# Sums of weights made by an adding DMA, and activation words turned by one DMA, in the feed-forward of a two-layer decoder on one Trainium2 core

## The chip, the cores and the metric

The kernel runs on one core of one Trainium2 chip. The metric is the device time of one execution in microseconds. In the trace PE is TensorE, PEld its weight load, DVE VectorE, ACT ScalarE, POOL GpSimd and SP SyncE; ACTq and SPq are DMAs being issued by ACT and by SP. PE ran at its full granted clock all through the profiled execution.

## The reference

Two pre-norm residual layers on 256 tokens of width 2048, each with an attention part and a SwiGLU feed-forward of width 5632. The change touches the feed-forward alone:

```python
def swiglu(h, w_gate, w_up, w_down):
    return (jax.nn.silu(h @ w_gate) * (h @ w_up)) @ w_down
```

Everything is float32. `h` is 256 x 2048, `w_gate` and `w_up` are 2048 x 5632, `w_down` is 5632 x 2048, for each of the two layers.

## The kernel before

**Products in three parts.** PE multiplies rounded 32-bit values. So each weight value and each activation is held as a high part (rounded, made by ACT, L1115) and a low part (what the rounding lost, made by DVE, L1379), and each product is three matmuls: high x high, high x low, low x high (`three`, L1757). ACT's and DVE's main work is this splitting of weights. A weight chunk of 128 x 2048 values (1 MB) comes into one of `RAW` = 4 slots of `raw`, and is split in halves of 128 x 1024 into a ring of `SPLIT` = 4 slots, `w_hi` and `w_lo`. ACT may write slot s when PE is done with the half that lies four back in the order; DVE follows ACT; SP loads a chunk into a `raw` slot when DVE is done with what was there. In the walk, the loop that all engines follow, the half that ACT splits at a step is `AHEAD` = 3 halves ahead of the one PE multiplies, and DVE's is 2 ahead.

**The feed-forward in column blocks.** `w_gate` and `w_up` are taken in 11 blocks of 512 columns. The first goes through two plain passes. For the other ten the two matrices go together: 8 chunks for each block, one for each pair k of row tiles (a, b), with up and gate side by side. The four 128 x 512 parts of a chunk lie as 0 = up rows a, 1 = gate rows a, 2 = up rows b, 3 = gate rows b. The body of a round takes them in the order k = 4, 5, 6, 7 of one block and then 0, 1, 2, 3 of the next (`BODY`). Six of the eight are "eights": two halves, 24 matmuls of 512 columns. Two, k = 4 (f = 0) and k = 7 (f = 1), are "sevens": the 2 x 2 blocks of weights are multiplied with seven products instead of eight, 21 matmuls, in four parts of 6, 3, 6 and 6 matmuls (`seven_part`, L1763). The parts need as weights: "two" = parts 2 and 3 of the chunk, "one" = part 1, "sums_a" = two sums, "sums_b" = the other two sums. The sums of weights are made by DVE in `make_sums` (L1382), in three steps: step 0 writes gate_a + up_a and up_b + up_a in one instruction (L1392) into `sums[2:4]`, which is "sums_b"; steps 1 and 2 (L1397) add up_b and then gate_b to the first of these, which gives "sums_a". The walk puts the steps ahead of the part that needs them: those of f = 0 at i = 4, 5, 6 of the four eights k = 0 to 3, those of f = 1 at i = 0, 1, 2 of the eights k = 5, 6. The matching sums of the activations (`form_hi`, `form_lo`) are made once for each layer. The seven products are put together again by ACT and DVE in `direct_out` and `mix`, during the second seven and the eights behind it. One round of the body (8 chunks, 186 matmuls of 512 columns) takes 44.2 us; there are nine such rounds in each layer, 18 in all.

**The hidden activations turned.** The result of a block, `hid`, must be turned for the product with `w_down`. DMAs turn 2-byte words only, so DVE splits the 4-byte values into two planes of words (`hidden_words`, L1707), ACT issues four transposing DMAs of 128 x 512 words each into `wordsT` (`hidden_turn`, L1344; L1350), and DVE merges the words into `hT` (`hidden`, L1717; L1722). In each round the turn stands at i = 3 of the eights k = 5, 6: in ACT's order it lies between the splits of "sums_a" and "sums_b" of the second seven. The memory of `words` is used again by ACT in `mix(0)`, which waits for the turn. There is one more turn behind the rounds of each layer and one in the first rows of the product with `w_down`.

**Other places that turn words.** In the attention parts SP issues transposing DMAs of 128 x 2048 words as one instruction (`turn_nat` L927, `turn_x` L939), which is the same size as the four of `hidden_turn` together.

**POOL** has little to do: small loads at the start, powers for the norms, and ten copies in the first layer's attention. In the rounds of the feed-forward it does nothing.

Of the kernel before, what the change touches and what calls it, by code (L numbers as in the profile page):

```python
# [22 lines left out]
P = 128  # L23
# [62 lines left out]
class Counts:  # L86


    def __init__(self):
# [6 lines left out]
        self.mix = Count()  # L96
        self.direct = Count()
# [15 lines left out]
    def loop(self, eng, rounds, sets=(0, 0), **per):  # L113

        known = {"half": self.half, "chunk": self.chunk, "made": self.made, "raw": self.raw, "up": self.up,
                 "sums": self.sums, "mix": self.mix, "direct": self.direct, "norm": self.norm, "qkT": self.qkT, "pair": self.pair,
# [97 lines left out]
def decoder_kernel(nc, widths, x_in, attn_norm, ffn_norm, even_w_in, even_q_norm, even_k_norm, even_sinks,  # L214
# [27 lines left out]
    with ExitStack() as ctx:  # L242
# [14 lines left out]
        with ExitStack() as s0:  # L257
            sums = sb("sums", [P, 4, NB], F32, s0)
        with ExitStack() as s1:
# [6 lines left out]
            wordsT = sb("wordsT", [P, 2, 4, SEQ], U16, s1)  # L266
            form_hi = sb("form_hi", [P, len(SEVENS), 4, P], F32R, s1)
            form_lo = sb("form_lo", [P, len(SEVENS), 4, P], F32R, s1)
        shared = words[:, :, :, :].rearrange("p w m n -> p (w m n)").bitcast(F32).rearrange("p (m n) -> p m n", n=NB)
        xs_sum = sums[:, 0:2, :].rearrange("p f (t s) -> p f t s", t=2)  # L270
        forms = sums[:, 2:4, :].rearrange("p f (c q) -> p f c q", q=P)
# [18 lines left out]
        bias = sb("bias", [P, 2, 2, S384], F32)  # L290
        t_two = sb("t_two", [P, 2, S384], F32)
        tri_r = sb("tri_r", [P, P], F32R)
        n_wordsT = sb("n_wordsT", [P, 2, MT, 4, P], U16)
# [29 lines left out]
        up_loaded = [sem(f"up_loaded{i}") for i in range(4)]  # L323
        sums_made = sem("sums_made")
# [108 lines left out]
        def split_views(kind, s, r):  # L433
# [7 lines left out]
            if kind in ("sums_a", "sums_b"):  # L441
                at = 0 if kind == "sums_a" else 2
                return HALF, sums[:, at:at + 2, :].rearrange("p a n -> p (a n)")
            return HALF, chunk[:, (r % 2) * HALF:(r % 2 + 1) * HALF]

        def split_over(n, kind):
# [3 lines left out]
            if kind != "plain":  # L450
                n.up.c += raw_halves

# [3 lines left out]
        def walk(eng, e):  # L456
# [151 lines left out]
            def feed_forward(layer):  # L608
# [38 lines left out]
                def make_sums(step, f, more):  # L647
                    e.sums(step, f, more)
# [23 lines left out]
                def sums_ahead(i):  # L672
                    if i in (4, 5, 6):
                        make_sums(i - 4, 0, 1 if i == 4 else 0)

                def body(j, more):

                    def middle(i):
                        if i < 3:
                            make_sums(i, 1, 1 if i == 0 else 0)  # L680
# [5 lines left out]
                    def tail(i):  # L686
# [3 lines left out]
                        if more:  # L690
                            sums_ahead(i)
# [9 lines left out]
                eights(range(FIRST_K), PARTS["seven"][:AHEAD], sums_ahead)  # L701
                with n.loop(eng, FB - 3, half=len(KINDS), made=len(KINDS), raw=16, up=16, sums=2, mix=1, direct=1, sets=(0, 2),
# [179 lines left out]
        def _(sp):  # L882
# [14 lines left out]
            def pair_chunk(layer, k, cols, halves, freed):  # L897
# [5 lines left out]
                for w, of, loaded in ((1, w_gate, raw_loaded[s]), (0, w_up, up_loaded[u])):  # L903
                    sp.dma_start(dst[:, w, :, :],
                                 of[layer][rows, cols].rearrange("(t p) n -> p t n", p=P)).then_inc(loaded, 16)
                n.chunk.c += 1
                n.up.c += 1
                n.half.c += halves
# [62 lines left out]
            def feed_forward(layer):  # L971
# [4 lines left out]
                for k in range(FIRST_K):  # L976
                    pair_chunk(layer, k, slice(NB, 2 * NB), 2, 2 * (RAW - 1))
                with n.loop(sp, FB - 2, chunk=8, up=8, half=whole) as j:
                    for i, of in enumerate(BODY):
                        k = (FIRST_K + i) % len(BODY)  # L980
                        freed = begins[i] - ends[i - RAW] + (whole if i < RAW else 0)
                        pair_chunk(layer, k, bass.ds(j * NB + (NB if k >= FIRST_K else 2 * NB), NB), len(PARTS[of]), freed)
                for k in range(FIRST_K, KT // 2):
                    pair_chunk(layer, k, slice((FB - 1) * NB, FB * NB), 2, 2 * (RAW - 1))
# [65 lines left out]
        def _(pool):  # L1050
# [41 lines left out]
            e = Steps(begin=begin, rms=rms, norm_b=norm_b, nat_words=nat_words)  # L1092
# [4 lines left out]
        def _(act):  # L1097
            def split(kind="plain"):
# [11 lines left out]
                if kind in ("sums_a", "sums_b"):  # L1110
                    act.wait_ge(sums_made, n.sums.value(unit=3))
                if n.made.past(SPLIT):
                    act.wait_ge(half_used, n.made.value(1 - SPLIT))
                out, src = split_views(kind, s, r)
# [871 lines left out]
```

## Time and profile before

| | us |
|---|---|
| median of 3 runs | 2169.42 (2167.51 to 2169.66) |
| the profiled execution, own time | 2165.94 |
| its span, first to last instruction | 2163.8 |
| PE busy | 2125.5 (98%) |
| DVE busy | 1490.3 (69%) |
| ACT busy | 1190.5 (55%) |
| POOL busy | 65.6 (3%) |
| DMA queues together, share of the 16 engines' time | 63.6% |
| moved by DMA | 442.35 MB |
| chain that ended last | PE 92%, ACTq 4%, DVE 2%, ACT 1% |

A matmul of 512 columns is shown with 389 ns, but one begins every 0.227 us: they overlap, and a busy PE here is a PE whose matmuls follow each other without a gap. Busy shares of the other engines say little, since each only has to keep ahead of PE.

### The profile page before, as it was taken

The page shows a single profiled execution, that of the slowest core. Times are in us where ns is not written, and L with a number is a line of the kernel's source. Part 1 is how long each engine was busy: PE and PEld are TensorE (multiplying, and loading weights), DVE is VectorE, ACT ScalarE, POOL GpSimd, SP SyncE. Part 2 cuts the span into 40 slices and gives each one's busy share as a digit, 9 for nine tenths or more (in the row PEclk, how much of TensorE's full clock was granted, in tenths as well). Part 3 has the DMA queues.
Part 4 walks back from the last instruction along what each step waited for, and adds up shares of the span by engine and source line. Part 5 has one row for each costly group of instructions (what it writes and reads, how often), then busy time and mean ns, then how long its engine had stood idle before and what let it go on. Part 6 is the DMA issues. An engine that isn't in the chain of part 4 may idle for free.

```text
span 2163.8 us, 28900 instructions
## 1 busy us (share of the span) xinstructions
PE 2125.5 (98%) x9859; PEld 1750.9 (81%) x9859; DVE 1490.3 (69%) x1957; ACT 1190.5 (55%) x1630; POOL 65.6 (3%) x39
## 2 busy tenths in 40 slices
PE   9999999999999999999999999999999999999999
PEld 8888888777777778888888888888777777788887
DVE  5775667788788766555667676776788878865555
ACT  6676656455554544444557576664555545544443
POOL 1101000000000000000011001000000000000000
PEclk9999999999999999999999999999999999999999
DMA  7776456656666576555567777765666665665553
GB/s 277 226 225 208 166 184 206 203 195 206 191 208 209 186 203 210 192 192 192 179 210 236 232 226 241 237 206 196 193 206 208 197 213 185 214 206 194 193 193 136
DMA packets 301851, 442.35 MB, mean 204 GB/s; under 512 B 134640, under 2 KB 137424, under 8 KB 291024
## 3 DMA queue, kind: packets, MB, share of 16 engines
q1 hardware_dynamic: 253488, 429.76, 60.4%
q10 hardware_dynamic: 47968, 11.58, 3.1%
q8 instruction: 46, 0.75, 0.1%
q14 instruction: 29, 0.24, 0.0%
q0 software_dynamic: 320, 0.02, 0.0%
HBM read 408.27 MB, written 2.10 MB: 190 GB/s over the span
## 4 chain that ended last, share of the span: by engine, by line
PE 92%; ACTq 4%; DVE 2%; ACT 1%; issue 0%; DMA 0%; SPq 0%; DVEq 0%
PE acc L1759 16%; PE acc L1760 15%; PE acc L1761 15%; PE work L1759 14%; PE work L1761 14%; PE work L1760 14%; ACTq L1350 4%; DVE w_lo L1379 1%; PE work L1909 1%; ACT w_hi L1115 1%; PE work L1947 1%; PE work L1859 0%; DMA raw<-in_even_w_in_dram 0%; PE work L1920 0%; PE work L1954 0%
## 5 line engine op out<-in xcount | busy, mean ns | idle before, releaser
L1115 ACT ACTIVATE w_hi<-raw 128x1024 fp32r<-128x1024 f32 x756 | 777.3, 1039 | 589.3 <-PE work L1761 360.1
L1379 DVE TENSOR_TENSOR w_lo<-raw,w_hi 128x1024 fp32r<-128x1024 f32 x756 | 897.0, 1196 | 178.9 <-ACT w_hi L1115 176.0
L1759 PE MATMUL work<-w_hi,xT_hi 128*128 128x512 f32 x1064 | 414.5, 390 | 0.0
L1761 PE MATMUL work<-w_hi,xT_lo 128*128 128x512 f32 x1064 | 414.2, 389 | 0.0
L1760 PE MATMUL work<-w_lo,xT_hi 128*128 128x512 f32 x1064 | 414.2, 389 | 0.0
L1759 PE MATMUL acc<-w_hi,xT_hi 128*128 128x512 f32 (+1 forms) x836 | 325.6, 389 | 1.1 <-DVE w_lo L1379 1.1
L1761 PE MATMUL acc<-w_hi,xT_lo 128*128 128x512 f32 (+1 forms) x836 | 322.2, 385 | 0.0
L1760 PE MATMUL acc<-w_lo,xT_hi 128*128 128x512 f32 (+1 forms) x836 | 322.1, 385 | 0.0
L1759 PEld LDWEIGHTS work<-w_hi,xT_hi 128*128 128x128 f32 x1064 | 200.0, 188 | 42.0 <-DVE w_lo L1379 0.4
L1760 PEld LDWEIGHTS work<-w_lo,xT_hi 128*128 128x128 f32 x1064 | 200.0, 188 | 41.7
L1761 PEld LDWEIGHTS work<-w_hi,xT_lo 128*128 128x128 f32 x1064 | 199.9, 188 | 41.6
L1759 PEld LDWEIGHTS acc<-w_hi,xT_hi 128*128 128x128 f32 x836 | 157.0, 188 | 36.7 <-DVE w_lo L1379 3.0
L1379 DVE TENSOR_TENSOR w_lo<-sums,w_hi 128x1024 fp32r<-128x1024 f32 x72 | 88.2, 1226 | 139.5 <-ACT w_hi L1115 138.2
L1761 PEld LDWEIGHTS acc<-w_hi,xT_lo 128*128 128x128 f32 x836 | 157.1, 188 | 31.8
L1760 PEld LDWEIGHTS acc<-w_lo,xT_hi 128*128 128x128 f32 x836 | 157.2, 188 | 30.2
L1115 ACT ACTIVATE w_hi<-sums 128x1024 fp32r<-128x1024 f32 x72 | 76.4, 1061 | 184.5 <-PE work L1761 105.1
L1728 DVE TENSOR_TENSOR stage_lo<-hT,stage_hi 128x256 fp32r<-128x256 f32 x88 | 37.4, 425 | 156.5 <-ACT stage_hi L1359 156.5
L1759 PE MATMUL work<-w_hi,stage_hi 128*128 128x512 f32 x352 | 137.2, 390 | 0.5 <-DVE hid L1702 0.5
L1759 PE MATMUL acc<-w_hi,stage_hi 128*128 128x512 f32 x352 | 137.0, 389 | 0.1
L1761 PE MATMUL work<-w_hi,stage_lo 128*128 128x512 f32 x352 | 137.0, 389 | 0.0
L1760 PE MATMUL acc<-w_lo,stage_hi 128*128 128x512 f32 x352 | 137.0, 389 | 0.0
L1761 PE MATMUL acc<-w_hi,stage_lo 128*128 128x512 f32 x352 | 136.9, 389 | 0.0
(176 smaller groups left out, 2420.2 us busy)
## 6 DMA issues: line engine op xcount, KB each, us to landing
raw<-in_ffn_w_down_dram SPq DMA_DIRECT2D x88, 1024.0 KB, 4.8
raw<-in_ffn_w_gate_dram SPq DMA_DIRECT2D x160, 512.0 KB, 3.6
raw<-in_ffn_w_up_dram SPq DMA_DIRECT2D x160, 512.0 KB, 4.5
raw<-in_odd_w_in_dram SPq DMA_DIRECT2D x48, 1024.0 KB, 5.6
raw<-in_even_w_in_dram SPq DMA_DIRECT2D x32, 1024.0 KB, 5.7
raw<-in_even_w_out_dram SPq DMA_DIRECT2D x16, 1024.0 KB, 5.0
raw<-in_odd_w_out_dram SPq DMA_DIRECT2D x16, 1024.0 KB, 5.8
bias<-in_bias_dram SPq DMA_DIRECT2D x24, 384.0 KB, 3.7
```

What stands on the lines that cost most here:

```text
L1115: act.activation(w_hi[:, s, 0:out], src, ACT.Copy).then_inc(hi_ready, 1)
L1350: act.dma_start_transpose(wordsT[:, w, :, m * P:(m + 1) * P], words[:, w, m, :]).then_inc(wordsT_loaded, 16)
L1379: dve.tensor_tensor(w_lo[:, s, 0:out], src, w_hi[:, s, 0:out].bitcast(F32), ALU.subtract).then_inc(lo_ready, 1)
L1728: dve.tensor_tensor(stage_lo[:, t, :], hT[:, bass.ds(kt, 1), :].rearrange("p a b -> p (a b)"), stage_hi[:, t, :].bitcast(F32), ALU.subtrac ...
L1759: pe.matmul(out_ps, x_hi, wh, start=start, stop=False)
L1760: pe.matmul(out_ps, x_hi, wl, start=False, stop=False)
L1761: return pe.matmul(out_ps, x_lo, wh, start=False, stop=stop)
L1909: last = pe.matmul(o[rows[b], m, :], v_nat[:, k, h * HD:(h + 1) * HD], pt[:, b, (k + m) * P:(k + m + 1) * P], start=first, stop=stop)
L1947: last = pe.matmul(banks[:, b, lo:hi], qT[rows[b], j % 4, m * P:(m + 1) * P], kT[rows[b], key, 0:hi - lo], start=True, stop=True)
```

## The change

Two independent edits, both in the feed-forward.

First, `hidden_turn` issues one transposing DMA of 128 x 2048 words instead of four of 128 x 512. The destination `wordsT` is laid out (plane, token tile, feature tile, token) to suit, and `hidden` reads it in that order.

Second, the two sums of "sums_b" are made by DMA. For a seven SP no longer loads up_a into `raw`; it loads gate and up_b as before, and loads gate_a and up_b once more into a buffer of their own, `near[f]`. POOL waits for these two loads and issues a DMA that reads up_a twice from the weights in memory and adds it to both parts of `near[f]`. "sums_b" is split from `near[f]`. DVE's step 0 is gone; its step 1 waits for the adding DMA and makes up_b + (gate_a + up_a) into `far[1]`, step 2 adds gate_b into `far[0]`, and "sums_a" is split from `far`. The buffer `bias` moves behind `tri_r` in memory.

```diff
@@ hidden_turn, hidden (ACT, DVE)
-                for w in range(2):
-                    for m in range(MT):
-                        act.dma_start_transpose(wordsT[:, w, :, m * P:(m + 1) * P],
-                                                words[:, w, m, :]).then_inc(wordsT_loaded, 16)
+                act.dma_start_transpose(wordsT[:, :, :, :, :].rearrange("p w m t q -> p (w m t) q"),
+                                        words[:, :, :, :].rearrange("p w m n -> p (w m n)")).then_inc(wordsT_loaded, 16)
@@
-                    last = dve.tensor_copy(pairs.rearrange("p (n w) -> p n w", w=2)[:, :, w],
-                                           wordsT[:, w, :, :].rearrange("p a q -> p (a q)"))
+                    last = dve.tensor_copy(whole[:, :, :, :, w], wordsT[:, w, :, :, :].rearrange("p m a q -> p a m q"))
@@ pair_chunk (SP)
+                if of == "eight":
+                    sp.dma_start(dst[:, 0, :, :],
+                                 w_up[layer][rows, cols].rearrange("(t p) n -> p t n", p=P)).then_inc(up_loaded[u], 16)
+                else:
+                    a, b = (slice((2 * k + t) * P, (2 * k + t + 1) * P) for t in range(2))
+                    f = SEVENS.index(k)
+                    sp.dma_start(dst[:, 0, 1, :], w_up[layer][b, cols]).then_inc(up_loaded[u], 16)
+                    sp.wait_ge(flo_ready, layer + 1)
+                    sp.dma_start(near[:, f, 0, :], w_gate[layer][a, cols]).then_inc(near_loaded[f], 16)
+                    sp.dma_start(near[:, f, 1, :], w_up[layer][b, cols]).then_inc(near_loaded[f], 16)
@@ POOL
+            def add_near(step, j, more, layer):
+                if step == 0:
+                    f, at = e.n.sums.slot(2), 2 * SEVENS[e.n.sums.slot(2)] * P
+                    pool.wait_ge(near_loaded[f], e.n.sums.turn(2, plus=1, unit=32))
+                    pool.nop(nofuse=True)
+                    pool.dma_start(near[:, f, :, :],
+                                   w_up[layer][at:at + P, bass.ds(j * NB + NB, NB)].unsqueeze(1).broadcast_to([P, 2, NB]),
+                                   accum_op=ALU.add).then_inc(near_added[f], 16)
@@ make_sums (DVE)
-                if step == 0:
-                    dve.wait_ge(lo_ready, n.made.value((-7, -3)[f]))
-                    dve.wait_ge(flo_ready, n.ffn.value())
+                if step == 1:
+                    dve.wait_ge(lo_ready, n.made.value(-(7, 3)[f] - 1))
+                    dve.wait_ge(near_added[f], n.sums.turn(2, plus=1, unit=16))
                     dve.wait_ge(raw_loaded[n.raw.slot(2 * RAW, more) // 2], n.raw.turn(2 * RAW, more, plus=1, unit=16))
                     dve.wait_ge(up_loaded[n.up.slot(2 * RAW, more) // 2], n.up.turn(2 * RAW, more, plus=1, unit=16))
-                    dve.tensor_tensor(sums[:, 2:4, :], chunk[:, 1:3, :],
-                                      chunk[:, 0:1, :].broadcast_to([P, 2, NB]), ALU.add).then_inc(sums_made, 1)
-                else:
-                    dve.wait_ge(sums_made, n.sums.value(unit=3) + step)
-                    out, a, b = ((1, sums[:, 2, :], chunk[:, 2, :]), (0, sums[:, 1, :], chunk[:, 3, :]))[step - 1]
-                    dve.tensor_tensor(sums[:, out, :], a, b, ALU.add).then_inc(sums_made, 1)
+                    dve.tensor_tensor(far[:, 1, :], near[:, f, 0, :], chunk[:, 2, :], ALU.add).then_inc(sums_made, 1)
+                if step == 2:
+                    dve.wait_ge(sums_made, n.sums.value(unit=2) + 1)
+                    dve.tensor_tensor(far[:, 0, :], far[:, 1, :], chunk[:, 3, :], ALU.add).then_inc(sums_made, 1)
```

## Rows read from the trace of the kernel before

**Rows 1.** The page's part 1, the engine line of PE.
```profile
PE 2125.5 (98%) x9859; PEld 1750.9 (81%) x9859; DVE 1490.3 (69%) x1957; ACT 1190.5 (55%) x1630; POOL 65.6 (3%) x39
```

**Rows 2.** Groups by line: busy us, mean ns | idle before, releaser.
```profile
L1759 PE MATMUL acc<-w_hi,form_hi 128*128 128x512 f32 x108 | 44.3, 411 | 31.7 <-DVE w_lo L1379 31.7
...
L1392 DVE TENSOR_TENSOR sums<-raw 128x1024 f32<-128x1024 f32 x36 | 43.9, 1219 | 0.0
```

**Rows 3.** Waits of PE, whole span: us in total, times, longest.
```profile
PE acc L1759 <- DVE w_lo L1379: 32.8, 20, 1.9
```

**Rows 4.** Timeline, one turn: start us, us, engine, line, operation [idle before].
```profile
539.49 5.19 ACTq L1350 DMA_TRANSPOSE wordsT<-words  x4
...
541.66 0.39 PE L1761 MATMUL work<-w_hi,xT_lo 128*128 128x512 f32 x1
...
544.80 1.06 ACT L1115 ACTIVATE w_hi<-sums 128x1024 fp32r<-128x1024 f32 x1 [4.38 <-PE acc L1761]
...
545.89 1.23 DVE L1379 TENSOR_TENSOR w_lo<-sums,w_hi 128x1024 fp32r<-128x1024 f32 x1 [4.21 <-ACT w_hi L1115]
...
547.17 0.50 PE L1759 MATMUL acc<-w_hi,form_hi 128*128 128x512 f32 x1 [1.72 <-DVE w_lo L1379]
```

**Rows 5.** Line L1350: issue ns shortest/median/longest, first and last start.
```profile
L1350 ACTq DMA_TRANSPOSE wordsT<-words x88: 1207/1299/1859, 406.8 to 1933.0; - x88
```

**Rows 6.** Line L927, SP's wide turns of the same size, same columns.
```profile
L927 SPq DMA_TRANSPOSE n_wordsT<-sq x13: 1322/1615/6267, 89.2 to 1336.9; - x13
```

**Rows 7.** Timeline of SP around a slow and a fast wide turn.
```profile
109.59 0.45 SPq L893 DMA_DIRECT2D raw<-in_even_w_in_dram  x1
110.39 5.88 SPq L927 DMA_TRANSPOSE n_wordsT<-sq  x1
...
1193.01 1.32 SPq L927 DMA_TRANSPOSE n_wordsT<-sq  x1
```

**Rows 8.** Timeline of SP through one round of the body.
```profile
506.48 0.37 SPq L904 DMA_DIRECT2D raw<-in_ffn_w_gate_dram  x1
...
510.30 0.37 SPq L904 DMA_DIRECT2D raw<-in_ffn_w_gate_dram  x1
...
518.37 0.37 SPq L904 DMA_DIRECT2D raw<-in_ffn_w_gate_dram  x1
...
538.97 0.37 SPq L904 DMA_DIRECT2D raw<-in_ffn_w_gate_dram  x1
539.44 0.42 SPq L904 DMA_DIRECT2D raw<-in_ffn_w_up_dram  x1
```

**Rows 9.** DMA issues: count, KB each, median us from issue to landing.
```profile
raw<-in_ffn_w_gate_dram SPq DMA_DIRECT2D x160, 512.0 KB, 3.6
raw<-in_ffn_w_up_dram SPq DMA_DIRECT2D x160, 512.0 KB, 4.5
...
sinks<-in_even_sinks_dram POOLq DMA_DIRECT2D x1, 8.0 KB, 5.5
```

**Rows 10.** Timeline of DVE from the sums of f = 0 to their split.
```profile
518.12 0.69 DVE L1397 TENSOR_TENSOR sums<-sums,raw 128x512 f32<-128x512 f32 x1
...
524.82 1.23 DVE L1379 TENSOR_TENSOR w_lo<-sums,w_hi 128x1024 fp32r<-128x1024 f32 x1
...
534.58 0.68 DVE L1397 TENSOR_TENSOR sums<-sums,raw 128x512 f32<-128x512 f32 x1
```

**Rows 11.** Timeline of PE: the first matmul that needs "sums_a" of f = 0.
```profile
528.28 0.39 PE L1759 MATMUL work<-w_hi,xT_hi 128*128 128x512 f32 x1
```

**Rows 12.** Timeline of POOL and DVE: a DMA issue, and POOL beside DVE.
```profile
6.07 0.58 POOL L1060 DMA_DIRECT2D sinks<-in_even_sinks_dram  x1
...
350.14 1.22 DVE L1379 TENSOR_TENSOR w_lo<-raw,w_hi 128x1024 fp32r<-128x1024 f32 x1
...
350.31 1.60 POOL L1066 TENSOR_TENSOR rstd<-msq,half 128x2 f32<-128x2 f32 x1 [142.29 <-DVE msq L1550]
...
1077.83 0.70 POOL L1066 TENSOR_TENSOR rstd<-msq,half 128x2 f32<-128x2 f32 x1 [725.91 <-DVE msq L1550]
```

More of the change, by code:

```diff
@@ L96, in __init__ @@
         self.mix = Count()
+        self.unit = Count()
         self.direct = Count()
@@ L257, in decoder_kernel @@
         with ExitStack() as s0:
-            sums = sb("sums", [P, 4, NB], F32, s0)
+            near = sb("near", [P, 2, 2, NB], F32, s0)
         with ExitStack() as s1:
@@ L323, in decoder_kernel @@
         up_loaded = [sem(f"up_loaded{i}") for i in range(4)]
+        near_loaded = [sem(f"near_loaded{i}") for i in range(2)]
+        near_added = [sem(f"near_added{i}") for i in range(2)]
         sums_made = sem("sums_made")
@@ L440, in split_views @@
                 return NB, chunk[:, NB:HALF]
-            if kind in ("sums_a", "sums_b"):
-                at = 0 if kind == "sums_a" else 2
-                return HALF, sums[:, at:at + 2, :].rearrange("p a n -> p (a n)")
+            if kind == "sums_a":
+                return HALF, far[:, :, :].rearrange("p a n -> p (a n)")
+            if kind == "sums_b":
+                return HALF, near[:, unit, :, :].rearrange("p a n -> p (a n)")
             return HALF, chunk[:, (r % 2) * HALF:(r % 2 + 1) * HALF]
@@ L451, in split_over @@
                 n.up.c += raw_halves
+            if kind == "sums_b":
+                n.unit.c += 1
         TURNS_B = ((19, (31, 32), 35, q_nat, qT, NA // 2), (32, (38, 39), None, k_nat, kT, NA // 2),
@@ L645, in stage, with make_sums @@
                     n.kt.c += 1
-                def make_sums(step, f, more):
-                    e.sums(step, f, more)
+                def make_sums(step, j, more):
+                    e.sums(step, j, more, layer)
                     if step == 2:
@@ L699, in body @@
                     n.sets[1].c += 2
-                eights(range(FIRST_K), PARTS["seven"][:AHEAD], sums_ahead)
-                with n.loop(eng, FB - 3, half=len(KINDS), made=len(KINDS), raw=16, up=16, sums=2, mix=1, direct=1, sets=(0, 2),
+                eights(range(FIRST_K), PARTS["seven"][:AHEAD], lambda i: sums_ahead(0, i))
+                with n.loop(eng, FB - 3, half=len(KINDS), made=len(KINDS), raw=16, up=16, sums=2, unit=2, mix=1, direct=1, sets=(0, 2),
                             hT=1) as j:
@@ L895, in chunk, with pair_chunk @@
                 n.half.c += 2
-            def pair_chunk(layer, k, cols, halves, freed):
+            def pair_chunk(layer, k, of, cols, freed):
                 sp.wait_ge(lo_ready, n.half.value(-freed))
@@ L902, in pair_chunk @@
                 rows = slice(2 * k * P, (2 * k + 2) * P)
-                for w, of, loaded in ((1, w_gate, raw_loaded[s]), (0, w_up, up_loaded[u])):
-                    sp.dma_start(dst[:, w, :, :],
-                                 of[layer][rows, cols].rearrange("(t p) n -> p t n", p=P)).then_inc(loaded, 16)
+                sp.dma_start(dst[:, 1, :, :],
+                             w_gate[layer][rows, cols].rearrange("(t p) n -> p t n", p=P)).then_inc(raw_loaded[s], 16)
+                if of == "eight":
[8 more added lines that the diff above has]
+                    sp.dma_start(near[:, f, 1, :], w_up[layer][b, cols]).then_inc(near_loaded[f], 16)
                 n.chunk.c += 1
                 n.up.c += 1
-                n.half.c += halves
+                n.half.c += len(PARTS[of])
             def columns(w, cols, which=range(KT // 4), after=None):
@@ L976, in feed_forward @@
                 for k in range(FIRST_K):
-                    pair_chunk(layer, k, slice(NB, 2 * NB), 2, 2 * (RAW - 1))
+                    pair_chunk(layer, k, 'eight', slice(NB, 2 * NB), 2 * (RAW - 1))
                 with n.loop(sp, FB - 2, chunk=8, up=8, half=whole) as j:
@@ L1110, in split @@
                 if kind in ("sums_a", "sums_b"):
-                    act.wait_ge(sums_made, n.sums.value(unit=3))
+                    act.wait_ge(sums_made, n.sums.value(unit=2))
                 if n.made.past(SPLIT):
                     act.wait_ge(half_used, n.made.value(1 - SPLIT))
-                out, src = split_views(kind, s, r)
+                out, src = split_views(kind, s, r, n.unit.slot(2))
                 act.activation(w_hi[:, s, 0:out], src, ACT.Copy).then_inc(hi_ready, 1)
```

41 lines of the change are left out of this document (22 added, 19 removed).

## The prediction

> **What bounds the kernel now.** First the busy times: PE is busy for 98% of the span [rows 1], and its clock is full throughout, so only two things can make the kernel faster: fewer matmuls, which this change does not bring, or the 2163.8 - 2125.5 = 38.3 us in which PE stands still. Second, the groups by line say where these are: 31.7 of the 38.3 us lie before the matmuls `acc<-w_hi,form_hi`, and DVE's low part L1379 ends them [rows 2]. PE's list of waits says the same, 32.8 us in 20 waits, the longest 1.9 us [rows 3]. There are 18 rounds of the body, and 31.7 / 18 = 1.76 us each; the round in the rows has 1.72 us. Third, the timeline of that round shows whose fault it is [rows 4]. ACT begins to issue the four turns at 539.49 and is done at 544.68. The last matmul of the half before ends at 541.66 + 0.39 = 542.05, and this frees the slot for "sums_b" of the second seven. But ACT starts that split only at 544.80, DVE follows at 545.89 and PE at 547.17. So what PE waits for is ACT's issuing of four DMAs in the middle of the seven, where a round has its least slack: the parts ahead of the last have only 6 + 3 + 6 matmuls. It is no shortage of VectorE and none of data.
>
> **The turn.** The four issues take 5.19 us, 1.30 each by the median of 88 [rows 4, 5]. One wide turn of the same 128 x 2048 words takes SP 1.6 us by the median of 13 [rows 6]. ACT would be free at 539.49 + 1.62 = 541.1, which is before the slot comes free at 542.05. Then the split of "sums_b" runs from 542.1 to 543.2 and its low part to 543.2 + 1.23 = 544.4. PE wants it when 15 matmuls of 0.227 us, begun at 541.66 + 0.22 = 541.88, are over: 545.3. So 0.9 us are left and the whole gap goes: -31.7 us. The issue may take up to 542.05 - 539.49 = 2.6 us at no cost, and up to 3.4 us before PE notices it. Next late behind it would be the copies of `direct_out` and the two halves after the seven; ACT has 1.0 us of work for each of these and PE 2.7 us, so nothing follows. The last turns of each layer lie beside eights, where PE shows no wait, and bring nothing. The merge `hidden` has as many elements as before and lies beside the eights too: 0.
>
> **DVE's step 0.** It goes away 36 times, 43.9 us of DVE [rows 2]. No wait of PE ends on it, for the only large one goes back to ACT's issues. I cost it at 0, not at -43.9. What it does bring is 1.1 us of slack for step 1 of f = 0.
>
> **SP.** Each seven has two more DMAs to issue, about 0.42 us each (0.42 is that of up in [rows 8]). The f = 0 chunk is issued at 506.48 and SP next acts at 510.30 [rows 8]; four issues end at 508.4. Queued behind are the weights of the next eight, needed over 15 us later. The wait for `flo_ready` is past before SP reaches the first seven of a layer. Cost 0.
>
> **The new wait.** DVE's step 1 now waits for the adding DMA, and everything DVE does stands behind it: `mix`, the splits of "two", "one", "sums_a" and "sums_b" of the first seven, and through them PE. Limit: in the trace step 1 of f = 0 starts at 518.12, and the low part of "sums_a" that is needed soonest starts at 524.82 and ends at 526.05 [rows 10]; PE takes it up at 528.28 [rows 11]. DVE is without a pause between, so step 1 may slip by 528.28 - 526.05 = 2.2 us, to 520.4. Supply, by steps: gate lands 3.6 us after its issue at 506.48, at 510.1, and up, issued 0.47 us later (the distance of 538.97 and 539.44), 4.5 us after that, at 511.45 [rows 8, 9]: 512 KB behind others take 1.37 us. A seven has 256 KB more in that row, + 0.7, so `near` is there at 512.1. Then the adding DMA. The trace has no accumulating one and no large one from POOL, so I bound it. Low: 3.6 us, the landing of 512 KB from SP, which gives 515.7. High: 5.5 us, the landing of POOL's `sinks` beside heavy loads [rows 9], plus 1.37 us for the data, plus 1.37 us if the destination must be read first, plus 0.9 us if DVE holds POOL up, as it did with `rstd`: 1.60 us where it started beside a two-input DVE instruction, 0.70 without [rows 12]. That is 9.1 us and gives 521.2. The middle, 518.5, is 1.9 us inside the limit; I take it, because most of the high end's terms lie on top of a landing measured in the busiest stretch of the run. Low end of the cost 0 us, high end 521.2 - 520.4 = 0.8 us a round, 14 us in all. For f = 1 the chunk is issued at 518.37 and step 1 stands at 534.58 [rows 8, 10]: 16.2 us where f = 0 has 11.6, so it cannot be late. POOL itself has nothing else queued there but the powers of the next norm.
>
> The Trainium skill's page "SBUF — State Buffer" ("Who interferes with whom") says that VectorE in a two-port mode locks GpSimd out and starves the descriptors of a DMA that GpSimd issues, while an instruction with two inputs in SBUF only holds up one of GpSimd that reads SBUF. The work of DVE at that time is of the second kind, so by the page the 0.9 us would fall away; `rstd`, which reads, agrees with it, and no row shows a DMA. Its page "DMA: Bandwidth & Descriptors" ("Anatomy of one DMA") gives 2.0 us plus bytes / 436 GB/s for a DMA from GpSimd, an estimate of 3.2 us here and of no cost at all.
>
> **Traffic.** A seven moves 1.75 instead of 1 MB (or 2.25 with the destination read). The next eight's load may land 1.4 to 2.7 us later, with over 10 us in hand. Cost 0.
>
> **Sum.** Span 2163.8 - 31.7 = 2132.1; around it lie 2165.9 - 2163.8 = 2.1 us: 2134.2 for the profiled execution. That one is 3.5 us below the median of the runs, 2169.42, so for the median 2169.4 - 31.7 = 2137.7: I say 2138. Its own range is 2133 to 2143.
>
> **Rivals.**
> 1. The wide turn is not issued in 1.6 us. SP's slowest wide turn took 6.27 us, and the one in the rows with 5.88 us was issued 0.35 us behind the end of a load's issue; the one at 1193.01, with no load close before it, took 1.32 us [rows 6, 7]. In the body the turn follows SP's loads of 538.97 and 539.44 just as closely [rows 8]. If it's the DMA engines that hold such a turn up, ACT stands still for about as long as it does now, 5.2 to 6.3 us: 0 to 1.1 us more a round than before, 2169 to 2189 us, about 2179. Against it: there the load was in the same queue, while here the queue is ACT's own, and the small turns, with the same loads in flight, never took over 1.86 us [rows 5]. Chance 0.15.
> 2. The adding DMA comes a little too late for f = 0: a stall of up to 1.7 us a round, 2139 to 2168 us. Chance 0.09.
> 3. The slower side: the adding DMA is so late that PE's new stall in front of "sums_a" of f = 0 is larger than the old gap. It decides at 520.4 + 1.76 = 522.2, that is 10.1 us after `near` is there. The mechanism would be that POOL cannot write its descriptors while DVE is without a pause, which lasts until DVE itself comes to step 1, at 518.1 at the latest: 518.1 + 0.6 for the issue [rows 12] + 5.5 is 524.2, a stall of 3.8 us, 18 x 3.8 = 68 us: 2138 + 68 = 2206 us. With the lower landing of 3.6 us it is 522.3, a stall of 1.9 us and 2172 us. For it speaks `rstd` beside DVE [rows 12], against it that `rstd` lost 0.9 us, one instruction's length, and not more. Chance 0.08.
> 4. Both edits do nothing that PE sees, because another wait of ACT (the copies of `direct_out`) takes the gap's place: 2169 us. The slack above speaks against it. Chance 0.03.
>
> **How the numbers follow.** The forecast has 0.65. About 0.2% or 4.3 us is what a measurement can tell from no change. Faster by more: the forecast, nearly all of rival 2 and a little of rivals 1 and 3, 0.74. Within it: the lower end of rivals 1 and 3, rival 4: 0.08. Slower: 0.18. The range for 8 in 10 takes in the forecast, rival 2 and the low end of rival 1: 2133 to 2172.
>
> **What would show it.** Right: L1350 with 18 + 4 turns of 1.3 to 2 us; no idle time before `acc<-w_hi,form_hi`; a round of 42.5 us in place of 44.2; PE's waits for L1379 near 1 us in all; step 1 of f = 0 starting before 520.4 counted from a chunk issued at 506.48, whatever DVE waits there. Wrong: turns of 5 us (rival 1), or idle time of PE in the first seven or before it, with DVE idle in front of step 1 on the adding DMA (rivals 2 and 3). The span would be off, too, if instructions of POOL slowed DVE's.

## The result, and the profile after

| | before | after |
|---|---|---|
| median of 7 runs, lowest to highest | 2167.51 us (2166.72 to 2169.90) | 2177.62 us (2172.26 to 2188.96) |
| span of the profiled execution | 2163.8 us | 2170.6 us |
| PE busy | 2125.5 us | 2128.2 us |
| DVE busy | 1490.3 us | 1453.7 us |

The ratio is 1.0046, interval 1.0026 to 1.0066: the changed kernel is slower by about half a per cent, where 1.4% faster was forecast. The profiled execution of the changed kernel is the fastest of its seven: its span is 6.8 us over that of before, while the medians differ by 10.1 us. What follows accounts for the 6.8. Nothing went wrong with what was taken off DVE, which is 36.6 us lighter. The page's part 1 of the changed kernel, then PE's list of waits (us in total, times, longest), which answers to [rows 1, 3]:

```profile
PE 2128.2 (98%) x9859; PEld 1753.2 (81%) x9859; DVE 1453.7 (67%) x1921; ACT 1193.1 (55%) x1630; POOL 108.8 (5%) x75
```
```profile
PE acc L1783 <- DVE w_lo L1404: 24.4, 15, 2.3
PE acc L1783 <- DVE stage_lo L1752: 10.8, 2, 5.5
...
PE work L1783 <- DVE w_lo L1404: 1.2, 1, 1.2
```

The wait that was to go, 32.8 us, is still 24.4 us in 15 places, 14 of them the gap in front of `form_hi`. A new one of 10.8 us stands in two places, and a third of 1.2 us in one. So PE's idle time went from 38.3 to 2170.6 - 2128.2 = 42.4 us, and its busy time rose by 2.7 us for the same 9859 matmuls. Together that is the 6.8 us of the span.

**The turn.** First the line of the turn, then its time to landing, which answer to [rows 5]; then the timeline of a round with a fast turn and of one with a slow turn, which answer to [rows 4]:

```profile
L1375 ACTq DMA_TRANSPOSE wordsT<-words x22: 1339/5082/5812, 406.4 to 1928.2; - x22
...
DMA to landing us min/median/max: 3.9/7.2/21.5
```
```profile
450.41 1.34 ACTq L1375 DMA_TRANSPOSE wordsT<-words  x1
...
453.01 1.06 ACT L1142 ACTIVATE w_hi<-near 128x1024 fp32r<-128x1024 f32 x1 [1.66 <-PE work L1785]
454.10 1.23 DVE L1404 TENSOR_TENSOR w_lo<-near,w_hi 128x1024 fp32r<-128x1024 f32 x1 [1.49 <-ACT w_hi L1142]
...
492.57 5.21 ACTq L1375 DMA_TRANSPOSE wordsT<-words  x1
...
497.90 1.06 ACT L1142 ACTIVATE w_hi<-near 128x1024 fp32r<-128x1024 f32 x1 [4.39 <-PE acc L1785]
498.99 1.23 DVE L1404 TENSOR_TENSOR w_lo<-near,w_hi 128x1024 fp32r<-128x1024 f32 x1 [4.22 <-ACT w_hi L1142]
...
500.27 0.50 PE L1783 MATMUL acc<-w_hi,form_hi 128*128 128x512 f32 x1 [1.74 <-DVE w_lo L1404]
```

In the second of these rounds one wide turn holds ACT for 5.21 us, where the four small ones held it for 5.19 [rows 4]. ACT splits "sums_b" at once when it is done, DVE follows, and PE has stood still for 1.74 us. In the round at 450.41 the issue takes 1.34 us. The split then follows 2.60 us after the turn's start, as soon as PE frees the slot, and the gap is gone. Of the 18 turns in rounds 4 are that short: the second, sixth, fourteenth and eighteenth of ACT's 22, late ones counted. That is why the wait fell only from 32.8 to 24.4 us.

How long is a long one? It ends just before SP's loads are there. The load that SP issued 0.2 us ahead of the turn at 492.57, and its time to landing:

```profile
492.37 0.42 SPq L913 DMA_DIRECT2D raw<-in_ffn_w_up_dram  x1
...
DMA to landing us min/median/max: 5.6/5.6/5.6
```

So it landed at 497.9, and the turn's issue ended at 492.57 + 5.21 = 497.78. In all 14 long turns of this trace the issue ends 0.13 to 0.19 us before the last of SP's loads that were in flight lands. In the short ones it does not wait: there the load lands some 4 us after the issue is over.

**The late turns.** The last two turns of each layer lie beside `w_down`'s 1 MB loads, as before. Here is the second one of the first layer:

```profile
819.88 2.07 ACTq L1375 DMA_TRANSPOSE wordsT<-words  x1
...
841.43 1.35 DVE L1747 COPY hT<-wordsT 128x1024 uint16<-128x1024 uint16 x2 [10.51 <-DMA wordsT<-words]
...
843.02 0.42 ACT L1384 ACTIVATE stage_hi<-hT 128x256 fp32r x1 [8.62 <-DVE hT L1747]
...
843.81 0.42 DVE L1752 TENSOR_TENSOR stage_lo<-hT,stage_hi 128x256 fp32r<-128x256 f32 x1
...
844.28 0.80 PE L1783 MATMUL acc<-w_hi,stage_hi 128*128 128x512 f32 x1 [5.53 <-DVE stage_lo L1752]
```

The issue is short, but the data lands 21.5 us later. DVE stands before the merge `hidden` for 10.51 us, ACT behind it, and PE for 5.53. The landing is slow on both sides: SP's five `w_down` loads issued in the same 34 us (812 to 846) took 15.2 us by the median, where the seven of before took 4.9. Below are first the loads of after, then those of before:

```profile
DMA to landing us min/median/max: 4.8/15.2/18.3
```
```profile
DMA to landing us min/median/max: 4.7/4.9/5.7
```

**The clock.** In the windows view (stretch, length, busy and instructions of PE, PEld, DVE, ACT, POOL, then granted clock, DMA share, GB/s), this is what came behind that stop:

```profile
839.00:844.00 5.00, 0.00 (x0) 0.00 (x0) 2.57 (x4) 0.98 (x2) 0.00 (x0) 0.98 0.75 297
844.00:849.00 5.00, 4.72 (x15) 3.83 (x16) 3.97 (x5) 1.93 (x4) 0.00 (x0) 0.67 0.54 179
```

PE stood still through the first window, and in the second the granted clock is 0.67: part of it at 1.2 GHz, the rest at 2.4. The matmuls at 844 take 0.63 us instead of 0.39. In the 60 us from 800 on, before does 262 matmuls and after 232. At 0.227 us each the 30 that are missing are 6.8 us. In the second layer it is 264 (1905 to 1965) against 231 (the same stretch): 7.5 us. So the late turns cost 14.3 us and the rounds gave back 4 x 1.75 = 7.0 us by their gaps; the 0.5 us between their difference and the 6.8 us of the span is what the late sum, the clock elsewhere and the matmuls behind the gaps come to together.

**The adding DMA.** The line of its issue, its time to landing, what DVE waited for it, and the timeline of one f = 0:

```profile
L1115 POOL DMA_DIRECT2D near<-in_ffn_w_up_dram x36: 1179/1194/1277, 375.1 to 1852.9; - x36
...
DMA to landing us min/median/max: 5.8/6.2/8.7
```
```profile
DVE far L1418 <- DMA near<-in_ffn_w_up_dram: 26.7, 20, 3.9
```
```profile
503.75 0.37 SPq L910 DMA_DIRECT2D raw<-in_ffn_w_gate_dram  x1
...
505.22 0.38 SPq L921 DMA_DIRECT2D near<-in_ffn_w_up_dram  x1
...
510.16 1.19 POOL L1115 DMA_DIRECT2D near<-in_ffn_w_up_dram  x1 [29.56 <-DMA near<-in_ffn_w_up_dram]
...
516.45 0.69 DVE L1418 TENSOR_TENSOR far<-near,raw 128x512 f32<-128x512 f32 x1 [1.27 <-DMA near<-in_ffn_w_up_dram]
```

POOL finds `near` loaded and starts its DMA 6.4 us after the chunk's first issue, and step 1 starts at +12.7. The limit that the prediction set is +13.9. In 15 of the 18 rounds step 1 starts at +14.3 or earlier, in the first of each layer at +16.1 without waiting for the DMA, and PE shows nothing. In the one of 1527 it starts at +15.3, and PE loses the 1.2 us of the third wait.

### The profile page after: what moved, and what is told of

Same layout as the page of the kernel before. It is cut to its first block, busy times and chain, and to the rows that moved or that the text cites. A ratio compares the mean times of both kernels' runs of the same rounds, so it can differ in the third digit from the quotient of the medians.

```text
span 2170.6 us, 29108 instructions
## 1 busy us (share of the span) xinstructions
PE 2128.2 (98%) x9859; PEld 1753.2 (81%) x9859; DVE 1453.7 (67%) x1921; ACT 1193.1 (55%) x1630; POOL 108.8 (5%) x75
## 4 chain that ended last, share of the span: by engine, by line
PE 89%; DMA 3%; ACTq 3%; DVE 2%; ACT 1%; issue 1%; SPq 0%; DVEq 0%; POOLq 0%
PE acc L1783 16%; PE acc L1785 15%; PE acc L1784 15%; PE work L1783 13%; PE work L1785 13%; PE work L1784 13%; ACTq L1375 3%; DMA wordsT<-words 2%; DVE w_lo L1404 1%; DMA near<-in_ffn_w_up_dram 1%; PE work L1933 1%; PE work L1971 1%; ACT w_hi L1142 1%; PE work L1883 0%; PE work L1944 0%
## 5 line engine op out<-in xcount | busy, mean ns | idle before, releaser
L1783 PE MATMUL acc<-w_hi,stage_hi 128*128 128x512 f32 x352 | 138.7, 394 | 10.8 <-DVE stage_lo L1752 10.8
L1784 PE MATMUL work<-w_lo,stage_hi 128*128 128x512 f32 x352 | 137.0, 389 | 0.0
L1783 PE MATMUL acc<-w_hi,oT_hi 128*128 128x512 f32 x256 | 100.7, 393 | 0.0
```

Of the source, the lines that this page charges most:

```text
L1783: pe.matmul(out_ps, x_hi, wh, start=start, stop=False)
L1784: pe.matmul(out_ps, x_hi, wl, start=False, stop=False)
```

## The experiments

In e1, e4, e5, e7, e8 and e9 the sums are made by DVE as before (there is no adding DMA). All runs have the new layout of `wordsT`. Every trace is of one execution, and where the executions of a kernel differ by many microseconds (e1, e2, e3), what is counted in its trace holds for that one.

**e1. The wide turn alone.** The kernel before with this edit and the merge that goes with it:

```diff
-                for w in range(2):
-                    for m in range(MT):
-                        act.dma_start_transpose(wordsT[:, w, :, m * P:(m + 1) * P], words[:, w, m, :])
+                act.dma_start_transpose(wordsT[...], words[...])    # one wide DMA
```

> The kernel before with the first edit alone: one wide turn issued by ACT, sums of weights still by VectorE. Theory A (the trace of the changed kernel read as it stands): the wide turn's issue holds ACT for about 5.1 us in most of the 18 rounds, as the four did, so most gaps of 1.7 us stay, and the last turn of each layer lands after some 20 us beside the loads of w_down and stops PE for 5.5 us, with a fall of the clock behind it: the same 5 to 12 us over the kernel before, 2172 to 2180 us. Theory B (the traffic of the sums made by DMA is what holds the turn): issue 1.6 us in every round, no late landing, 31.7 us less than before, 2136 us.

Measured: 2176.41 us (2173.08 to 2181.47), ratio 1.0042 [1.0030, 1.0054]. PE's waits:

```profile
PE acc L1757 <- DVE w_lo L1377: 26.9, 15, 2.4
PE acc L1757 <- DVE stage_lo L1726: 10.6, 2, 7.4
```

Both waits of after are here, and the issue is 5.28 us by the median. The slower time belongs to the turn.

**e2. The sums alone.** The changed kernel with the turn put back to four small DMAs on ACT; the layout of `wordsT` and the merge stay as changed.

> The changed kernel with the four small turns put back: the sums by loads and an adding DMA alone. Theory A: the adding DMA costs VectorE waits of 1 to 2 us for the sums of the first seven, which PE does not see but for one or two rounds, so within 3 us of the kernel before, 2166 to 2171 us, with PE's gaps of 1.7 us in all 18 rounds. Theory B: the traffic or the wait is what made the changed kernel slower: 2175 us or more.

Measured: 2185.03 us (2180.50 to 2194.19), ratio 1.0093 [1.0076, 1.0110]. PE's waits, and the landing of the adding DMA:

```profile
PE acc L1784 <- DVE w_lo L1405: 34.1, 20, 2.8
PE work L1784 <- DVE w_lo L1405: 7.6, 7, 1.5
```
```profile
DMA to landing us min/median/max: 5.8/6.3/10.1
```

The old gap is whole, and in 6 of the 18 rounds step 1 of f = 0 starts at +14.75 or later and PE stops before "sums_a" (0.60 us at +14.75, 1.50 at +15.90). With the four small turns the sums cost 17.7 us; beside the wide turn they cost 1 us or so (2177.62 against e1's 2176.41, each beside its own before). What separates the two in the traces is how many adding DMAs are late (6 rounds against 1), not a price of every DMA.

**e3. The late turns small.** The changed kernel, with the last two turns of each layer as four small DMAs again:

```diff
+                if late:
+                    for w in range(2):
+                        for m in range(MT):
+                            act.dma_start_transpose(wordsT[:, w, m, :, :], words[:, w, m, :])
+                    return
```

> The changed kernel, but with the last two turns of each layer, those behind the rounds, issued as four small ones again. Theory A: the 5.5 us stop of PE at the start of the product with w_down goes in both layers, with the slow clock behind it, together 13.7 us by the windows of the trace; what stays is the saving of the 4 rounds with a fast wide turn, about 7 us: 2160 to 2166 us. Theory B (the landing is late because of anything but the width): no change, 2177 us.

Measured: 2173.26 us (2163.56 to 2178.33), ratio 1.0020 [1.0005, 1.0035]. The stop on `stage_lo` is gone from PE's waits, but the time fell by only 4.4 us. The adding DMA now landed late in 11 of 18 rounds, and a stop before "sums_a" took the place of the one removed (before it, the changed kernel had 1.2 us in one place):

```profile
PE work L1791 <- DVE w_lo L1412: 14.6, 12, 1.5
```

So this run does not price the late turns; e9 does that, without the sums. Against e9 it shows a second price of the sums, 5.9 + 6.6 = 12.5 us, again beside a wide turn. The sums have no fixed price, then: 1 us, 12.5 and 17.7 in three surroundings, and 5.3 in a fourth (e6, below). This kernel's executions also lie 15 us apart, and the trace is of its slowest, so the 11 late rounds need not hold for the others.

**e9. The late turns small, without the sums.** The first experiment with the same edit: the wide turn in the 18 rounds only.

> The kernel before with the wide turn on ACT in the 18 rounds only; the last two turns of each layer stay four small ones, sums by VectorE. Theory A: of the 9 us that the wide turn alone cost, the late landing in front of w_down was more than all, and the wide turn in the rounds gains the gaps of the 3 or 4 rounds in which its issue is short (5 to 7 us) and nothing else: 2158 to 2166 us. Theory B: the wide issue costs in the rounds as well: 2170 us or more.

Measured: 2160.60 us (2158.32 to 2161.43), ratio 0.9968 [0.9956, 0.9979]; PE's only wait over 1.2 us is

```profile
PE acc L1765 <- DVE w_lo L1385: 24.9, 14, 2.0
```

Here 5 of the 18 turns are short, and they bring 5 x 1.75 = 8.8 us by the rows. By the waits it is 7.9, since the 13 gaps that stay are 1.82 to 2.03 us long. In the runs the wide turn in the rounds is worth -6.6 us, and its late landing costs 9.1 + 6.6 = 15.7 us (e1 against this run, each beside its own before), where the rows of after gave 14.3.

**e4. The turn issued by SP.** The kernel before with the wide turn in the rounds moved from ACT to SP, behind SP's last load of the round; late turns small on ACT:

```diff
-                        if i == 3:
-                            e.hidden_turn()
...
+                    sp.wait_ge(words_ready, n.hT.value(1))
+                    sp.dma_start_transpose(wordsT[...], words[...])    # one wide DMA
```

> The kernel before, with the rounds' turn as one wide DMA issued by SP behind its last load of the round, where SP stands idle for over 10 us; the last two turns of each layer stay four small ones on ACT; sums by VectorE. Theory A (the gap is ACT being held by issues, however they are cut): ACT's split of sums_b starts when its slot comes free, the gap before the matmuls on form_hi is gone in all rounds, 31 us less: 2133 to 2138 us, while SP's issue may take 5 to 6 us and hold nothing. Theory B (something else stands behind the ACT's issues and takes the gap's place): less than 10 us gained, 2158 us or more.

Measured: 2126.95 us (2126.31 to 2126.96), ratio 0.9814 [0.9801, 0.9826]. The line of the turn, its timeline in one round with ACT and DVE beside it, and the group of [rows 2] that held the 31.7 us:

```profile
L986 SPq DMA_TRANSPOSE wordsT<-words x18: 4387/4632/4845, 407.3 to 1830.9; - x18
```
```profile
533.78 4.79 SPq L986 DMA_TRANSPOSE wordsT<-words  x1
...
535.83 1.06 ACT L1122 ACTIVATE w_hi<-sums 128x1024 fp32r<-128x1024 f32 x1 [1.66 <-PE work L1771]
536.92 1.23 DVE L1389 TENSOR_TENSOR w_lo<-sums,w_hi 128x1024 fp32r<-128x1024 f32 x1 [1.49 <-ACT w_hi L1122]
```
```profile
L1769 PE MATMUL acc<-w_hi,form_hi 128*128 128x512 f32 x108 | 42.0, 389 | 0.0
```

The turn is nearly as slow as on ACT (4.63 us by the median, 5.28 in e1), but SP has nothing to issue until 542.28, and ACT splits "sums_b" the moment that PE frees the slot. The idle time before the group is 0.0. The 2.3 us that the group's own busy time lost (44.3 to 42.0) are matmuls behind the gap that took longer in the trace: 411 ns on average before, 389 now.

**e5. Four small turns issued by SP**, in the rounds; ACT keeps the late ones.

> As the run with the wide turn on SP (2126.95 us), but SP issues four small turns in each round. Theory A (only ACT's hold matters; SP has over 10 us to spare at that place): four issues of 1.3 us on SP, 5.2 us, the same time within 2 us, 2125 to 2129 us. Theory B (the wide turn itself brought part of the 40 us, by landing earlier): 2132 us or more.

Measured: 2126.30 us (2126.16 to 2127.42), ratio 0.9808 [0.9791, 0.9824]; the issues are 1.27 us each, 5.1 together. One wide or four small makes no difference once ACT is out of it: the ratios' intervals lie over each other. This is the fastest kernel of the study, by no more than its uncertainty. Theory B, that the earlier landing of the wide turn brought part of the gain, is out.

**e7. The turn in two halves on ACT.** The kernel before with `wordsT` turned by two DMAs of 128x1024 words.

> The kernel before with every turn issued by ACT as two DMAs of 128 x 1024 words. Theory A (an issue is long when one DMA has more descriptors than fit, so halves go through at once): two issues of 1.3 to 1.5 us, ACT held 2.6 to 3.0 us in each round, no gap before form_hi or one under 0.3 us, 2128 to 2135 us. Theory B (the issue waits for the data of the whole turn to move, however it is cut): 5 us in all for both, gaps of 1.7 us in most rounds, 2165 to 2178 us.

Measured: 2168.52 us (2163.71 to 2171.09), ratio 1.0002 [0.9993, 1.0012]. One round's issues, and the range of the single ones:

```profile
540.73 5.30 ACTq L1349 DMA_TRANSPOSE wordsT<-words  x2
```
```profile
L1349 ACTq DMA_TRANSPOSE wordsT<-words x44: 1248/1448/4232, 406.5 to 1932.7; - x44
```

In this round the first half takes 1.26 us and the second 4.02. So one, two and four DMAs of the same words hold ACT for 5.2, 5.3 and 5.2 us beside the loads. Fewer of them bring nothing here, but the sums have different terms. The wide turn and the second half are held until SP's loads are nearly there: in all 18 rounds of this trace the second half's issue ends 0.13 to 0.29 us before the landing. The four small ones are never held, each takes 1.3 us with the loads in flight, and 4 x 1.3 happens to be as long. No run had four small turns, or a wide one on ACT in the rounds, with nothing in flight.

The late turns of this kernel landed up to 15.8 us after their issue (the line's longest), and PE stopped on `stage_lo` for 2.5 us in two places. One, two and four DMAs there land after up to 21.5, 15.8 and 6.7 us: for the landing beside the 1 MB loads the width does count.

**e8. The SP turn with the loads landed.** As the SP version, but the turn waits until the low part of "sums_b" is made, 5 us after the last load's issue instead of 0.6 us.

> The wide turn on SP, but issued only when VectorE has made the low part of sums_b of the second seven, some 5 us later, when the loads of 538.97 and 539.44 (in the time of the kernel before) have landed. Theory A (loads in flight make the wide issue long): issue of 1.3 to 1.7 us and a landing of 3.7 to 4 us, against 4.6 and 6.7 us right behind the loads; the time stays near 2127 us. Theory B (the wide issue is long by itself beside a short ring): issue of 4 us or more there too.

Measured: 2127.46 us (2126.98 to 2127.54), ratio 0.9811 [0.9795, 0.9827]. The line of the turn:

```profile
L988 SPq DMA_TRANSPOSE wordsT<-words x18: 1560/1612/1649, 412.7 to 1835.9; - x18
```

4.63 us became 1.61, and the landing 3.7 instead of 6.7. In every round of e8 the loads had landed, 0.3 to 0.8 us before the turn began. In e4 they landed 4.6 to 5.0 us after it began, and each issue ended 0.10 to 0.21 us before that. The same instruction on the same engine is three times as long when two 512 KB loads are in flight. In the time nothing changes, since SP's occupation was covered in both.

**e6. The sums on top of the SP version.** The changed kernel with its rounds' turn on SP and the late ones small.

> The changed kernel with the rounds' turn issued wide by SP and the late turns small: sums by the adding DMA where ACT is never held. Theory A (the adding DMA lands now and then over 14.1 us after the gate load of the first seven was issued, and each such round costs PE 0.6 to 1.5 us, plus a slow clock behind some gaps): 3 to 30 us over the 2126.95 us of the same kernel with sums by VectorE, 2130 to 2157 us, and PE waits before the first seven in some rounds. Theory B (the sums by DMA cost only what ACT's hold made of them): 2127 us.

Measured: 2132.26 us (2131.68 to 2133.89), ratio 0.9835 [0.9819, 0.9852]: 5.3 us slower than the same kernel with DVE's step 0. PE stops on "sums_a" for 3.2 us in 3 places; two of the 18 adding DMAs of f = 0 are late and stop PE (step 1 at +15.9 and +16.7).

**e10. `near` loaded first.** The same kernel, with SP issuing `near`'s two loads ahead of the chunk's others, so that POOL may start sooner.

> As the sums by the adding DMA with the turn on SP (2132.26 us), but for a seven SP issues the two loads into near ahead of gate and up_b instead of behind them. Theory A (the 5 us over the kernel with sums by VectorE are PE's waits in rounds in which the adding DMA lands late): near is there about 1.4 us earlier, the adding DMA starts at 5 instead of 6.4 us after the first issue and no round is over 14.1 us: 2126 to 2129 us. Theory B (traffic or POOL's descriptors cost them): still 2131 us or more.

Measured: 2134.51 us (2132.14 to 2135.30), ratio 0.9852 [0.9837, 0.9867], no gain. POOL does start sooner, at about +4.1 instead of +6.4, but its DMA then runs beside the rest of the chunk, and step 1 of f = 0 starts at +13.7 or later in every round:

```profile
DMA to landing us min/median/max: 5.6/8.4/11.5
```

**e11. Copying instead of adding.** The kernel with the sums and the SP turn, but POOL's DMA overwrites `near` with `up_a` instead of adding it: the two sums lack the term that was loaded there. All loads, bytes from memory and waits stay.

> As the sums by the adding DMA with the turn on SP (2132.26 us), but POOL's DMA only copies up_a to both halves of near and adds nothing; so the sums lack one term, and the rest of the work is the same. It measures what the adding itself costs. Theory A (an adding DMA has to read its destination first): the landing falls from 6.2 us and up to 9.5 to 4.5 us or less, step 1 is never late, 2126 to 2129 us. Theory B (it is POOL's issue and the loads beside it, not the adding): landing of 5.8 us or more as before, and 2131 us or more.

Measured: 2127.27 us (2126.97 to 2127.45), ratio 0.9817 [0.9802, 0.9832], equal to the version without the sums within the uncertainty. In one round step 1 still starts at +14.9, and PE loses 0.7 us. POOL's issue and the landing:

```profile
L1122 POOL DMA_DIRECT2D near<-in_ffn_w_up_dram x36: 722/722/787, 375.4 to 1817.5; - x36
...
DMA to landing us min/median/max: 3.9/4.8/7.0
```

Against e6 the adding takes 0.47 us more of issue and 1.5 us more of median landing (6.3 us there). The 5.0 us in time between this run and e6 are the price of the adding itself, not of the two loads more in each seven.

## Why the prediction was wrong, point by point

- **PE is the bound, and the 31.7 us are ACT's issuing.** Right. The turn moved off ACT removes exactly this gap (31.7 to 0.0). By its own measure the step was too small: 2167.3 - 2127.0 = 40.4 us came back, where the idle time gave 38.3 - 6.0 = 32.3. The rest is PE's busy time, 2125.5 to 2118.9 us. What a gap costs beyond its length shows when the same matmuls are compared, from the last one before the gap to the tenth behind it: first in before, then in e4.

```profile
545.06 0.39 PE L1761 MATMUL acc<-w_hi,form_lo 128*128 128x512 f32 x1
...
549.36 0.39 PE L1759 MATMUL work<-w_hi,xT_hi 128*128 128x512 f32 x1
```
```profile
538.80 0.39 PE L1771 MATMUL acc<-w_hi,form_lo 128*128 128x512 f32 x1
...
541.07 0.39 PE L1769 MATMUL work<-w_hi,xT_hi 128*128 128x512 f32 x1
```

These take 4.30 and 2.27 us, so a gap of 1.73 us costs 2.03. In 17 of the 18 rounds the difference is 2.0 to 2.2 us. In the other it is 3.6, because there the clock fell behind the gap. Together that is 38.6 of the 38.9 us between the spans. The premise that the clock was full throughout, which also stands in the section on the chip, is therefore not quite right:

```profile
720.00:725.00 5.00, 3.19 (x14) 2.30 (x13) 2.17 (x2) 3.26 (x5) 0.00 (x0) 0.96 0.62 135
725.00:730.00 5.00, 5.00 (x17) 3.96 (x17) 3.80 (x5) 4.02 (x6) 0.00 (x0) 0.70 0.24 71
```

A granted clock of 0.70 is in part 1.2 GHz and in part 2.4, and only 17 matmuls fall into this stretch, where 5 us at 0.227 each hold 22.

- **"ACT would be free at 541.1."** This is the step that failed. The 1.6 us was the median of 13 turns of SP, most of them with no load just ahead. The right rows were in the same group. Three of the 13 turns begin within 0.6 us of the end of a load's issue, and they are the three longest: the 5.88 us of [rows 7] and these two.

```profile
158.90 0.43 SPq L893 DMA_DIRECT2D raw<-in_even_w_in_dram  x1
159.43 6.27 SPq L927 DMA_TRANSPOSE n_wordsT<-sq  x1
...
175.48 0.37 SPq L893 DMA_DIRECT2D raw<-in_even_w_in_dram  x1
176.38 5.23 SPq L927 DMA_TRANSPOSE n_wordsT<-sq  x1
```

The other ten begin 3.7 us or more behind and take 1.3 to 2.3 us. There was no spread around a median, but two cases. In the body the turn stands just as close behind two loads, and it takes 5.1 us by the median. That loads in flight are what makes it long is shown on SP, by e4 against e8 (4.63 and 1.61 us); on ACT the four late turns, 3 us behind the last load's issue, took 1.6 to 2.1 us. The prediction had this as rival 1, with 2169 to 2189 us and a chance of 0.15; 2177.62 is in that range. Its two reasons against were both too weak. That "the queue is ACT's own" did not help: beside loads that SP has issued ACT is held as long as SP is beside its own. That "the small turns never took over 1.86 us" is so, but it does not carry over to a wide one. The small ones are not held by the loads, and the wide one is. The two-halves run (1.26 and 4.02 us) shows the hold in the second DMA of a turn.
- **"The last turns bring nothing: 0."** This step failed too, and it is the larger loss: 14.3 us by the rows, 15.7 by runs. Only the issue was looked at, and that is short here (2.07 us). The landing was not costed. The question would have been what the merge `hidden` does when the turn lands late. Where rival 1 reached 2179 by longer issues of ACT, the real sum is a partial gain in the rounds and a loss in the late turns. So that the time fell into the range of rival 1 is in part luck: its mechanism holds, but in the rounds the wide turn came out 6.6 us below before (e9), and what brought the time up to 2177.62 is the late turns, which rival 1 did not have.
- **DVE's step 0 is worth 0.** Right. Its 43.9 us left DVE (36.6 net), and the version that has this saving at the lowest cost of transfer (2127.27) is no faster than the one without (2126.95).
- **SP, 0.** Right. The seven's four issues end 1.9 us after the first one's start, as forecast, and no wait ends on SP's issuing.
- **The new wait.** Its frame was right: `near` there at +5.6 forecast, POOL starting at +6.2 to +6.9 measured; landing within 3.6 to 9.1 us forecast, 6.2 us by the median; step 1 may slip to +13.9 forecast, while PE shows nothing at +14.3 and 0.60 us at +14.75. The middle of 518.5 (+12.0) was measured as +12.7. POOL's issue is 1.19 us, not the 0.58 of [rows 12]. What the middle hid is the spread: some of the adding DMAs take over 8 us to land, and where step 1 slips to +14.75 or later by it, PE lost 0.6 to 3.2 us. That was so in 1 round of 18 in the changed kernel, 2 in e6, 6 in e2 and 11 in e3. (Not every late one costs: the first round of each layer has room, and so had one round of e2 at +15.7.) Rival 2 (a stall of up to 1.7 us a round) came true in part. Rival 3, POOL kept from writing its descriptors, did not: POOL issues 0.6 to 1.3 us after the data was due by the forecast, and its 36 issues all take 1.18 to 1.28 us, so the 0.9 us for a POOL held up by DVE did not appear either.

The estimate of 3.2 us from the Trainium skill's page "DMA: Bandwidth & Descriptors" ("Anatomy of one DMA") does not hold for the adding DMA: 5.6 us is the shortest in any run. Even the copying one, with 3.9 us at the shortest and 4.8 by the median, is above it, beside other loads.

The same page ("Issuing engines are not separate DMA queues") says that spreading DMAs over engines saves only the time to initiate them, "which is usually small relative to the DMA itself". The first part agrees: moving the turn to SP hardly changed its landing (6.7 us by the median, 7.4 on ACT in e1). The size does not: the initiating is 5.2 of 7.2 us in the turn at 492.57, and taking it off ACT was worth 40 us, the whole gain of the study.

## What to carry over

Take an issue's duration from the row whose neighbours on the queues are those of the new place, not from the median, and cost the landing beside the issue. If the durations of one kind of row fall into two groups, look for what stands ahead of the long ones before taking a median. When an engine is held up by issuing DMAs, moving them to one that has nothing queued behind them was worth 40 us here, and making them fewer nothing. A DMA put in place of work on an engine that is not the bound has nothing to win and can lose: its median may be inside the slack while its tail is not.

## What was not expected of the hardware

- A transposing DMA of 128 x 2048 words held its issuing engine for 1.3 to 2.3 us when the last load had been issued 3 us or more before (1.6 us with the loads landed, e8), and mostly for 4.1 to 5.9 us right behind two 512 KB loads, even when another engine issued those. In the traces with wide or half turns there are 144 issues of over 3 us, on ACT and on SP, and 139 of them end 0.10 to 0.29 us before the last load in flight lands (the other five 1.7 to 1.8 us after it). In the rounds of before the small ones of 128 x 512 words took 1.2 to 1.4 us each beside the same loads. What the wide one waits for in the loads is open.
- On ACT every fourth turning DMA was short all the same (1.34 us at 450.41, 5.21 at 492.57): the second, sixth and so on of its queue wherever that one was a wide turn in a round, in all four kernels with the wide turn there, where in e3 and e9 the late turns count as four each. On SP none of 72 in four kernels was, and in e7 no second half was. The cause is open.
- One wide turn beside 1 MB loads landed after 21.5 us (23.4 in the turn-alone run), two halves after up to 15.8, where four small ones took at most 6.7 each, and the loads went from 4.9 to 15.2 us. Why the two hold each other up was not tried.
- Adding in a DMA is slower than copying: 1.19 against 0.72 us of issue and 6.3 against 4.8 us to landing for 512 KB (e6 and e11). Why it is late in so different a number of rounds (1 to 11 of 18 in single executions) stays open.
- Gaps of PE of 1.7 us and up are now and then followed by some microseconds at the lower clock: behind one of the 18 gaps in the rounds of before, and behind 5 of 14 in e1. So the price of a gap can be more than its length, and part of what separates the executions of one kernel may be that; it was not tried.
